# A two-block transformer forward: weight remainders of the experts on one engine, semaphores cleared by ranges

## What is computed

```python
def hier_moe(x, w_group, b_group, w_router, b_router, w_gate, w_up, w_down):
    logit_g = (xt @ w_group + b_group)            # 4 groups: softmax, best group
    ...
    logit_e = take_along_axis(xt @ w_router + b_router, g_sel)   # 4 experts of that group
    top_v, top_i = lax.top_k(jax.nn.softmax(logit_e, -1), 2)
    ...
    for g in range(4):                            # in effect: 2 of 16 experts for a token
        h = silu(einsum('nd,edf->nef', xt, w_gate[e])) * einsum('nd,edf->nef', xt, w_up[e])
        y = y + einsum('nef,efd->nd', h * combine[:, g], w_down[e])

def reference(x, ...):
    x = first_block(x, ...)     # x + diff_attention(rmsnorm(x)), then x + hier_moe(rmsnorm(x))
    return second_block(x, ...) # 2 layers: mixer, conv-gated feed-forward; final norm
```

## Time and profile before

| | us |
|---|---|
| median of 3 runs (1935.60 to 1937.38) | 1935.61 |
| the profiled execution, its own time | 1936.05 |
| the span of its trace | 1934.2 |
| TensorE busy in the span | 1799.9 (93%) |
| VectorE busy | 1072.3 (55%) |
| ScalarE busy | 914.9 (47%) |
| GpSimd busy | 792.4 (41%) |

### The profile page before, as it was taken

The page is one execution under the profiler, slowest core; times in us unless marked ns, Lnnn a source line. Parts: engine busy times, 40 slices in busy tenths (PEclk is TensorE's granted clock), DMA queues, the critical chain, the costliest instruction groups (busy, mean ns, idle before and its releaser), DMA issues.

```text
span 1934.2 us, 23827 instructions
## 1 busy us (share of the span) xinstructions
PE 1799.9 (93%) x8318; PEld 1420.8 (73%) x8318; DVE 1072.3 (55%) x1819; ACT 914.9 (47%) x1558; POOL 792.4 (41%) x413
## 2 busy tenths in 40 slices
PE   5999995899998399989999999999999999999995
PEld 4777765777777367667788888887776788888884
DVE  4455445999999358874555555223335555555121
ACT  5555543878777234434444444332446444444221
POOL 3222133666676132233344444443442344444441
PEclk9999997999999699999999999999999999999998
DMA  5332324899996222222222222333431223323331
GB/s 187 129 119 77 131 76 148 317 370 363 360 361 246 100 76 68 64 57 64 69 96 98 98 97 90 98 100 94 133 99 45 74 90 98 98 98 95 94 96 54
DMA packets 67130, 252.73 MB, mean 131 GB/s; under 512 B 12813, under 2 KB 16014, under 8 KB 54619
## 3 DMA queue, kind: packets, MB, share of 16 engines
q1 hardware_dynamic: 61962, 243.37, 37.4%
q0 software_dynamic: 5072, 8.11, 1.2%
HBM read 248.05 MB, written 15.29 MB: 136 GB/s over the span
## 4 chain that ended last, share of the span: by engine, by line
PE 53%; ACT 2%; DVE 1%; issue 0%; POOL 0%; DVEq 0%; ACTq 0%
PE ps L202 16%; PE ps L204 16%; PE ps L203 16%; PE ps L509 1%; PE ps L522 1%; PE ps L532 1%; ACT prob L642 1%; PE ps L560 1%; ACT probT L649 0%; PE ps L540 0%; DVE selb L1148 0%; DVE m L1147 0%; POOL ring_wl L269 0%; PE ps L555 0%; DVE fo L2544 0%
## 5 line engine op out<-in xcount | busy, mean ns | idle before, releaser
L269 POOL TENSOR_TENSOR ring_wl<-ring_w,ring_wh 128x1024 fp32r<-128x1024 f32 (+1 forms) x229 | 542.8, 2372 | 944.7 <-ACT ring_wh L261 944.7
L202 PE MATMUL ps<-two_x_high,ring_wh 128*128 128x512 f32 x1064 | 422.2, 397 | 0.0
L203 PE MATMUL ps<-two_x_low,ring_wh 128*128 128x512 f32 x1064 | 414.7, 390 | 0.0
L204 PE MATMUL ps<-two_x_high,ring_wl 128*128 128x512 f32 x1064 | 414.6, 390 | 0.0
L261 ACT CAST ring_wh<-ring_w 128x1024 fp32r<-128x1024 f32 (+1 forms) x229 | 235.1, 1029 | 205.4 <-PE ps L204 204.5
L202 PEld LDWEIGHTS ps<-two_x_high,ring_wh 128*128 128x128 f32 x1064 | 199.9, 188 | 50.1 <-issue 8.3
L203 PEld LDWEIGHTS ps<-two_x_low,ring_wh 128*128 128x128 f32 x1064 | 200.1, 188 | 42.9 <-issue 2.4
L204 PEld LDWEIGHTS ps<-two_x_high,ring_wl 128*128 128x128 f32 x1064 | 200.0, 188 | 42.0
L913 ACT ACTIVATE acc<-ps,param 128x512 f32<-128x512 f32 x88 | 68.6, 780 | 171.9 <-DVE ps L933 171.9
L202 PE MATMUL ps<-hid_high,ring_wh 128*128 128x512 f32 x352 | 136.9, 389 | 0.0
L203 PE MATMUL ps<-hid_low,ring_wh 128*128 128x512 f32 x352 | 136.9, 389 | 0.0
(11 more groups left out here) (311 smaller groups left out, 3323.3 us busy)
## 6 DMA issues: line engine op xcount, KB each, us to landing
ring_w<-in_w_ff_up SPq DMA_DIRECT2D x88, 512.0 KB, 3.6
one_wg<-in_w_gate SPq DMA_DIRECT2D x32, 1024.0 KB, 7.4
one_wu<-in_w_up SPq DMA_DIRECT2D x32, 1024.0 KB, 8.1
one_wd<-in_w_down SPq DMA_DIRECT2D x32, 1024.0 KB, 7.9
ring_w<-in_w_ff_down SPq DMA_DIRECT2D x32, 448.0 KB, 3.3
ring_w<-in_w_da SPq DMA_DIRECT2D x24, 512.0 KB, 3.6
ring_w<-in_w_ff_down SPq DMA_DIRECT2D x16, 512.0 KB, 3.5
ring_w<-in_w_rel SPq DMA_DIRECT2D x12, 512.0 KB, 3.6
```

The costliest lines, as they stand in the source:

```text
L202: mm(out, wh, xh, start=start, stop=False)
L203: mm(out, wh, xl, start=False, stop=False)
L204: return mm(out, wl, xh, start=False, stop=stop)
L269: self.c.nc.gpsimd.tensor_tensor(self.low[s][:, 0:k, :], self.slab[s][:, 0:k, :], self.high[s][:, 0:k, :].bitcast(F32), ALU.subtract).then ...
```

## The change

1. The low parts of all expert pieces are VectorE's. `BY_POOL` is gone, one semaphore `split` takes the place of two. In the loop VectorE does pieces 4 to 11 in one row. GpSimd keeps scatters and gathers.
2. Two pieces leave the routing chain: GpSimd's piece 5 of slot 0 (it goes to VectorE, behind the sort), and the third `idx` weight of the ring, whose rounding goes behind ScalarE's first expert pieces and whose remainder goes on GpSimd behind the gather for slot 1.
3. VectorE makes the tile list (`vector_sort`) ahead of the first expert pieces (`vector_first`), not behind three of them.
4. Three ring loads (`a0` + 0 to 2) go from ahead of the `hrows` store to the end of SyncE's block one.
5. A stage's semaphores are cleared by ranges of consecutive numbers.

```diff
--- before.py
+++ after.py
@@ -167,8 +167,13 @@
     def __exit__(self, *exc):
         if exc[0] is None:
+            nums = sorted(s.num for s in self.sems)
+            first = 0
+            for n in range(1, len(nums) + 1):
+                if n == len(nums) or nums[n] != nums[n - 1] + 1:
+                    self.nc.gpsimd.sem_clear(range(nums[first], nums[n - 1] + 1))
+                    first = n
             for s in self.sems:
-                self.nc.gpsimd.sem_clear(s)
                 self.nc.release_semaphore(s)
         return super().__exit__(*exc)
@@ -1610,7 +1615,7 @@
             sp.dma_start(self.c.a["hrows"][tt * P:(tt + 1) * P, :], self.buf["rows"][:, tt, :]).then_inc(self.stored, 16)
     def gpsimd(self, pool):
-        for m in range(DC):
+        for m in range(DC - 1):
             self.ring.rest(pool, self.j0 + m + 3)
     def tensor(self, pe):
@@ -1683,7 +1688,6 @@
         nc.scalar.activation(buf["rsc"][:, :], buf["rsl"][:, :], ACT.Exp, scale=-0.5).then_inc(self.rs_ok, 1)
         for i in range(5, 8):
             row(i)
-        ring.round(act, self.j0 + 10)
     def vector(self, dve):
         for m in range(DC):
@@ -1865,18 +1869,16 @@
-    def __init__(self, c, st, buf, route, gathered, scattered):
-        self.c, self.buf, self.route = c, buf, route
+    def __init__(self, c, st, buf, route, gathered, scattered, ring, ring_job):
+        self.c, self.buf, self.route, self.ring, self.ring_job = c, buf, route, ring, ring_job
         self.gathered, self.scattered = gathered, scattered
         self.w_in = [st.sem(f"moe_w_in{half}") for half in range(6)]
...
         self.slabs = {x: buf["w" + x] for x in "gud"}
-
-    BY_POOL = (5, 8, 11)
     def count(self, eng):
         eng.wait_ge(self.route.sorted, 1)
@@ -1896,23 +1898,18 @@
     def parted(self, i, k, end=False):
-        first = isinstance(i, int) and i == 0
-        before = sum(p in self.BY_POOL for p in range(8 if end else 0, k + 1))
-        if k in self.BY_POOL:
-            return self.split_p, (0 if first else 3 * i - 2) + before
-        return self.split_v, (0 if first else 9 * i - 2) + k + 1 - (8 if end else 0) - before
+        return self.split, self.nth(i, k, end) + 1
     def piece(self, k):
         if k < 8:
             return self.slabs["gu"[k // 4]][:, 2 * (k % 4):2 * (k % 4) + 2, :].rearrange("p a e -> p (a e)")
         return self.slabs["d"][:, k - 8, :]
-    def rest(self, eng, i, k, end=False):
+    def rest(self, dve, i, k, end=False):
         b = self.buffer(i, k, end)
-        eng.wait_ge(self.rounded, self.nth(i, k, end) + 1)
-        (self.c.nc.gpsimd if k in self.BY_POOL else self.c.nc.vector).tensor_tensor(
-            self.buf["wl"][b][:, :], self.piece(k), self.buf["wh"][b][:, :].bitcast(F32), ALU.subtract)\
-            .then_inc(self.split_p if k in self.BY_POOL else self.split_v, 1)
+        dve.wait_ge(self.rounded, self.nth(i, k, end) + 1)
+        self.c.nc.vector.tensor_tensor(self.buf["wl"][b][:, :], self.piece(k), self.buf["wh"][b][:, :].bitcast(F32),
+                                       ALU.subtract).then_inc(self.split, 1)
     def round(self, act, i, k, end=False):
         if k % 2 == 0:
@@ -1995,13 +1992,9 @@
         def body(i):
             if self.later(i, 2):
                 free_y(i - 2)
-            if self.later(i, 1):
-                self.rest(pool, i, 5)
             if self.later(i, 2):
                 scatter(i - 2)
             if self.later(i, 1):
-                self.rest(pool, i, 8)
-                self.rest(pool, i, 11)
                 gather(i + 2)
         for j in (2, 4):
@@ -2013,13 +2006,12 @@
         pool.wait_ge(stored, 16 * TT)
         pool.wait_ge(self.route.back, 16)
         gather(1)
+        self.ring.rest(pool, self.ring_job)
         gather(2)
         repeat(pool, self.count(pool), body, peel=2)
         l = self.last(pool)
         free_y(l - 1)
-        self.rest(pool, l + 1, 8, end=True)
         scatter(l - 1)
-        self.rest(pool, l + 1, 11, end=True)
         free_y(l)
         scatter(l)
         pool.wait_ge(self.scattered, 16 * l + 48)
@@ -2160,7 +2152,7 @@
         copy_y(l, self.nth(n, 4))
     def vector_first(self, dve):
-        for k in range(2, 5):
+        for k in range(2, 6):
             self.rest(dve, 0, k)
     def vector(self, dve):
@@ -2183,7 +2175,7 @@
                 for k in range(4):
                     self.rest(dve, i, k)
                 rest_h(i - 1)
-            for k in ((4,) if self.later(i, 1) else ()) + (6, 7) + ((9, 10) if self.later(i, 1) else ()):
+            for k in ((4, 5, 6, 7, 8, 9, 10, 11) if self.later(i, 1) else (6, 7)):
                 self.rest(dve, i, k)
             dve.wait_ge(self.silued, i + 1)
@@ -2199,7 +2191,7 @@
         repeat(dve, self.count(dve), body, peel=2)
         l = self.last(dve)
         rest_h(l)
-        for k in (9, 10):
+        for k in range(8, 12):
             self.rest(dve, l + 1, k, end=True)
@@ -2272,7 +2264,7 @@
         diff = Diff(c, st, ring, norms, buf)
         out = Outward(c, st, ring, norms, buf, None)
         route = Route(c, st, out, buf, listed)
-        experts = Experts(c, st, buf, route, gathered, scattered)
+        experts = Experts(c, st, buf, route, gathered, scattered, ring, at["idx"] + 2)
         out.experts = experts
         with nc.Block("one") as block:
@@ -2302,11 +2294,13 @@
                 ring.wait_used(sp, at["o"] - 1)
                 experts.load(sp, 0, 4, None, expert=0)
                 experts.load(sp, 0, 8, None, expert=0)
-                for m in range(6, DC + 6):
+                for m in range(6, DC + 3):
                     ring.load(sp, at["o"] + m)
                 out.store(sp)
                 route.read(sp)
                 experts.sync(sp)
+                for i in range(3):
+                    ring.load(sp, at["a0"] + i)
             @block.gpsimd
             def _(pool):
@@ -2314,7 +2308,6 @@
                     ring.rest(pool, i)
                 diff.gpsimd(pool)
                 out.gpsimd(pool)
-                experts.rest(pool, 0, 5)
                 route.gpsimd(pool)
                 experts.gpsimd(pool, out.stored)
@@ -2347,6 +2340,7 @@
                 out.scalar(act)
                 route.scalar(act)
                 experts.scalar_first(act)
+                ring.round(act, at["idx"] + 2)
                 experts.scalar(act)
             @block.vector
@@ -2364,8 +2358,8 @@
                 diff.vector(dve)
                 out.vector(dve)
                 route.vector(dve)
+                route.vector_sort(dve)
                 experts.vector_first(dve)
-                route.vector_sort(dve)
                 experts.vector(dve)
```

4 lines of the change are left out of this document (2 added, 2 removed).

## The result

| | us |
|---|---|
| changed kernel, median of 4 runs (1902.58 to 1907.92) | 1906.8 |
| kernel before, median of 4 runs beside it (1935.6 to 1937.38) | 1936.05 |
| ratio | 0.984 (95%: 0.983 to 0.985) |
| the changed kernel's profiled execution, its own time and span | 1907.92, 1906.0 |
| changed kernel again, with other kernels, 5 runs (1904.53 to 1908.59) | 1905.49 |

It is faster, by 29.3 us in the first measurement and 31.2 us in the second (ratio 0.984, 0.983 to 0.986). The forecast was 35.4 us less, with 1895.5 to 1910 as its range. The stated range holds both medians, but the gain is 6.1 us smaller than forecast in the first measurement and 4.2 us in the second. Lines of the code have moved: the remainders' line 1913 is 1911 now, the list scatters' 1729 is 1733, the products' 202 to 204 are 207 to 209.

A forecast was written before the change was run, and what follows sets the result against it. VectorE was taken to bound the loop, with TensorE 4% away. Gains of 14.0 + 2.2 + 1.2 + 2.7 + 7.0 + 8.3 = 35.4 us gave 1900.2 us against the median of 1935.61; range 1895.5 to 1910.

The forecast's parts named there:

- rival B: In the experts' loop: busy DMA engines (0.98) keep it short of TensorE's bound, 18.4 us a slot, 1908.9 us; chance 13%.
- What bounds the loop: Bodies 2 to 15: VectorE, slowed beside GpSimd's pieces, is the bound; afterwards TensorE is, 17.75 us a body, 14.0 us gained.
- After the loop: Behind the loop: VectorE does the last piece 8 in 1.21 us, where GpSimd took 2.34; 1.2 us gained.
- Clears: Border and end: a range clear costs the same as a single one, 68 ns; 7.0 and 8.3 us gained.
- Routing, up to the list: Routing chain: two instructions slowed beside GpSimd's remainders become quick, and the copy of positions starts 3.2 us earlier.
- Routing, the scatters: Routing chain: list scatters lengthen beside VectorE's pieces, costing some 0.5 us, so body 1 starts 2.7 us earlier.
- Rival C: In the loop: GpSimd's index copy waits for VectorE's whole row of eight pieces, 4 us a body, 1956 us; chance 5%.
- Slot 1: Loop, body 1: from first matmul to turn takes 11.05 us without a break, against 13.23; 2.2 us gained.
- The signs it named: Profile after: equal piece times, no TensorE waits in bodies 2 to 15, quick routing instructions, short border wait and end.

## Why the prediction was right, and where it was off

The mechanisms of the loop and of the clears were right, and they are nearly all of the gain. That the median lies in the stated range is in part luck: the forecast's own range was 1896 to 1904.5 us, and both medians, 1906.8 and 1905.49, lie above it. The range to 1910 was there for rival B, and it was not rival B that used it but the scatters, slot 1 and the clock.

- **What bounds the loop: right.** VectorE and GpSimd held each other up: without GpSimd's pieces the down pieces take 1.22 us like the others, the break is gone, the slot is 17.71 us (17.75 predicted). The 14 slots gave 14.6 us where 14.0 were predicted (column e). VectorE's busy time was put at 16.2 us a slot and is 16.4; one piece more fits and two don't.
- **After the loop: right.** TensorE's wait there was 5.10 us and is 3.9, 1.2 us less. In the changed kernel's two profiles 0.5 and 0.7 us of it are lost again in the matmuls behind it, which have the low clock for longer.
- **Clears: right.** 7.0 + 8.3 predicted, 6.3 + 8.3 in the marks, 15.8 in the medians. The step that a clear over a range costs what a single one costs had no row behind it, as the prediction said, and held.
- **Routing, up to the list: right.** 3.2 us predicted, 3.1 measured where the clock doesn't dip.
- **Routing, the scatters: the step that failed.** "with four pieces behind the short sort, one more half does, some 0.5 us" took the 1.85 us of the earlier trace rows as the price of any scatter beside any run of pieces. It was 3.65 us: one scatter of 5.21 and one of 1.85. With that, the chain's 2.7 us of gain are a loss of 0.4 in the changed kernel's second profile (turn at 335.72, before 335.36). Holding the pieces back gives 4.9 us. Rival C named this mechanism, at the wrong place: in the changed kernel's loop, where VectorE stops for ScalarE between pieces, GpSimd's copy takes 0.35 us and its scatter 1.7. Its argument against itself, these stops, was right: one and two more pieces close some of them, and the copy takes 3.3 us and the scatter 7.37. At the place with the longest unbroken row of pieces, ahead of slot 0, I had counted the overlap and not asked who would be next.
- **Slot 1: right mechanism, size open to chance.** 2.2 us predicted, 2.2 measured at full clock (17.36 against 19.58). With the low clock slot 1 takes 18.9 to 20.1 us, and the gain is gone. Of ten profiles with the loop's edit and a slot as short, six have the low clock. In all fourteen the clock is low at the turn of slot 1's rows, whose eight transposes last 1.97 us there and 1.03 later; what differs is when it returns, by 340 us in the kernel before and only at 344 to 346 us in the changed kernel's second profile. In the kernel before it costs nothing: 19.33 us with it and 19.58 without, since VectorE was the bound there and TensorE only waited less.
- **The clock ahead of it: not in the sum.** Two places, 3.2 us together, in some executions and not in others. The profile of before happened to have neither, and the sum was made against it.
- **The signs it named.** One duration for all pieces, no waits of TensorE, turns 17.7 us apart and the quick routing instructions came. SyncE's wait at the border is 0.7 us, not under 0.5, and the span ends 1.2 us behind the last landing, not within 1. The turn of slot 1's rows, put at 332.7, came at 339.55 and 335.72.

Together, for the second profile of the changed kernel, whose span is 30.6 us shorter than that of the kernel before: first scatter -3.1, scatters +3.65, slot 1 -0.3, slots -14.6, after the loop -1.2, the border's clears -6.3, from the border to the end -9.3, and the rest +0.5. Against the forecast's 35.4 this lacks 3.15 us at the scatters, 1.9 in slot 1, and 0.7 each at the border's clears and in the matmuls behind the loop (at the low clock for longer); the slots brought 0.6 more and the end 1.0.

## What to carry to other kernels

A large elementwise piece that moves off GpSimd leaves its small operations behind: ask of each, above all of indirect DMAs on the critical path, which unbroken row of the other engine's work it now meets, and bound it by the length of the whole row, not by one piece. Where the row isn't urgent, let it wait for the last of the small operations; here one wait is worth 4.9 us, as slot 0 had 13 us to spare. And when an engine becomes the bound, its own disturbances begin to count: a low clock that cost nothing in slot 1 costs 2 us afterwards.

## What the runs showed of the hardware that I had not expected

- An indirect DMA that GpSimd issues took 5.21, 5.19, 5.38 and 4.43 us beside four back-to-back subtractions of 128x1024 on VectorE, each time until some 0.85 us behind the end of the run, and 0.97 alone; beside six such in the loop it took 7.37. A copy of 128x2 numbers on GpSimd took 3.3 us in the same way, and 0.18 alone. With a wait between the subtractions, which spaced them 0.11 us further apart, the scatter took 1.81. The same four subtractions in another order of the program let it in after one.
- A clear of a range of semaphores costs no more than a clear of one: 6 ranges in place of 231 single clears save 15.8 us by the medians; 68 ns for each of the 225 would be 15.3.
- TensorE's granted clock fell to 1.2 GHz at 42 to 46 us in some profiles and stayed at 2.4 GHz in others, with the same instructions; likewise in slot 1, behind idle times of 3.5 to 13.1 us when low, and of 8.8 to 13.4 us when full. The length of the idle time alone doesn't tell.
